# Two-layer encoder block: the mixer's products from rows without the norm, and a convolution shared between VectorE and ScalarE

## What is computed

```python
def rms_norm(x, g):
    xf = x.astype(jnp.float32)
    y = xf * lax.rsqrt(jnp.mean(xf * xf, axis=-1, keepdims=True) + RMS_EPS)
    return (y * g.astype(jnp.float32)).astype(x.dtype)
...
  h = RMSNorm(x)
  one combined input projection of h -> columns partitioned into
    [diff-attn q | diff-attn k | diff-attn v | ssd z | ssd xBC | ssd dt (2 directions) | gate_attn | gate_ssd]
...
        q = rms_norm(q.reshape(b, s, ATTN_HEADS, 2, ATTN_HEAD_DIM), qk_norm_g[i, 0])
        k = rms_norm(k.reshape(b, s, ATTN_HEADS, 2, ATTN_HEAD_DIM), qk_norm_g[i, 1])
...
    u = lax.conv_general_dilated(xbc, conv_w.astype(xbc.dtype)[:, None, :], (1,), [(pad, pad)],
                                 dimension_numbers=("NWC", "WIO", "NWC"),
                                 feature_group_count=SSM_CONV_CH)
    u = jax.nn.silu(u + conv_b)
```

## Time and profile before

| | |
|---|---|
| median of 3 runs | 1735.32 us (1735.26 to 1735.81) |
| the profiled execution, its own time | 1734.33 us |
| its span, first to last instruction | 1732.5 us |
| PE busy | 1686.1 us, 97% of the span |
| DVE, ACT, POOL busy | 718.0, 683.6, 667.9 us (41, 39, 39%) |
| mixers (about) | 0 to 440 us and 867 to 1300 us |
| DMA mean rate | 305 GB/s; about 427 GB/s in the expert stages |

### The profile page before, as it was taken

The page is one execution under the profiler, slowest core; times in us unless marked ns, Lnnn a source line. Parts: engine busy times, 40 slices in busy tenths (PEclk is TensorE's granted clock), DMA queues, the critical chain, the costliest instruction groups (busy, mean ns, idle before and its releaser), DMA issues.

```text
span 1732.5 us, 23236 instructions
## 1 busy us (share of the span) xinstructions
PE 1686.1 (97%) x8975; PEld 1046.0 (60%) x8975; DVE 718.0 (41%) x1351; ACT 683.6 (39%) x1549; POOL 667.9 (39%) x536
## 2 busy tenths in 40 slices
PE   8999999999999999999899999999999999999997
PEld 6889877787434444343378898777874344444342
DVE  6728788524222222221176287875242222122121
ACT  5565787754211111111156557877541111111111
POOL 7788776895000000000077987768940000000000
PEclk9999999999999999999999999999999999999999
DMA  7454312766999999999954452227589999999997
GB/s 285 184 195 152 141 50 102 284 265 275 408 428 428 427 428 427 426 428 428 424 212 162 179 195 98 84 106 283 233 320 414 427 428 427 427 428 428 426 427 311
DMA packets 44659, 528.47 MB, mean 305 GB/s; under 512 B 4824, under 2 KB 7640, under 8 KB 12288
## 3 DMA queue, kind: packets, MB, share of 16 engines
q1 hardware_dynamic: 44512, 526.89, 74.1%
q0 software_dynamic: 32, 0.02, 0.0%
HBM read 525.82 MB, written 1.06 MB: 304 GB/s over the span
## 4 chain that ended last, share of the span: by engine, by line
PE 70%; DMA 13%; DVE 9%; ACT 5%; issue 2%; POOL 1%; SPq 0%; DVEq 0%; ACTq 0%
PE PS L1286 19%; DMA view<-in_w_exp_up_dram 12%; PE PS L1317 11%; PE PS L870 8%; PE PS L872 8%; PE PS L871 8%; DVE view L1987 5%; PE PS L1232 3%; PE PS L1218 2%; DVE view L1983 1%; PE PS L1077 1%; PE PS L1219 1%; ACT view L1555 1%; DMA wr<-in_w_router_dram 1%; PE PS L858 1%
## 5 line engine op out<-in xcount | busy, mean ns | idle before, releaser
L2368 POOL TENSOR_TENSOR view<-view,view 128x512 fp32r<-128x512 f32 x448 | 579.8, 1317 | 543.2 <-ACT view L1441 532.4
L1286 PE MATMUL PS<-view,view 128*64 128x512 f32 x2044 | 455.4, 595 | 19.2 <-DMA view<-in_w_exp_gate_dram 9.9
L1441 ACT ACTIVATE view<-view 128x512 fp32r<-128x512 f32 x448 | 274.5, 631 | 150.7 <-PE PS L872 147.7
L1286 PEld LDWEIGHTS PS<-view,view 128*64 128x64 f32 x2044 | 143.1, 137 | 301.3 <-issue 263.5
L870 PE MATMUL PS<-view,view 128*128 128x512 f32 x704 | 285.4, 405 | 5.1 <-POOL view L2368 3.2
L872 PE MATMUL PS<-view,view 128*128 128x512 f32 x704 | 275.1, 391 | 0.0
L871 PE MATMUL PS<-view,view 128*128 128x512 f32 x704 | 274.9, 391 | 0.0
L2268 DVE SCALAR_TENSOR_TENSOR view<-PS,gcol,view 128x512 fp32r<-128x512 f32 x64 | 48.0, 751 | 476.3 <-ACT view L1754 459.0
L1317 PE MATMUL PS<-view,stb 128*64 128x512 f32 x1024 | 227.7, 596 | 4.4 <-ACT stb L1730 1.5
L1317 PEld LDWEIGHTS PS<-view,stb 128*64 128x64 f32 x1024 | 70.3, 137 | 137.3 <-issue 125.6
L870 PEld LDWEIGHTS PS<-view,view 128*128 128x128 f32 x704 | 132.5, 188 | 32.6 <-issue 5.1
(11 more groups left out here) (263 smaller groups left out, 2028.1 us busy)
## 6 DMA issues: line engine op xcount, KB each, us to landing
view<-in_w_exp_up_dram SPq DMA_DIRECT2D x60, 2048.0 KB, 26.9
view<-in_w_exp_gate_dram SPq DMA_DIRECT2D x60, 2048.0 KB, 26.9
view<-in_w_mix_dram SPq DMA_DIRECT2D x54, 2048.0 KB, 7.6
view<-in_w_exp_down_dram SPq DMA_DIRECT2D x54, 2048.0 KB, 28.8
view<-in_w_exp_down_dram SPq DMA_DIRECT2D x16, 1024.0 KB, 23.9
view<-in_w_mix_dram SPq DMA_DIRECT2D x8, 512.0 KB, 17.9
view<-in_w_exp_gate_dram SPq DMA_DIRECT2D x2, 1792.0 KB, 9.4
view<-bias_table SPq DMA_DIRECT2D x2, 1536.0 KB, 11.8
```

The costliest lines, as they stand in the source:

```text
L1286: ins = pe.matmul(bank(ph, name, j)[e * CAP:(e + 1) * CAP, :], xgT1[:, k, at + e * CAP:at + (e + 1) * CAP], weight_rows(j, kind, row, 1), ...
L1441: nc.scalar.activation(highs(chunk), weights(slot8, chunk), ACT.Copy).then_inc(*high_ready.up(ph))
L2368: g_.tensor_tensor(weights(low8, chunk), weights(slot8, chunk), highs(chunk), ALU.subtract).then_inc(*low_ready.up(ph))
```

## The change

The transposes take the rows of X as they are, so that r is not needed before the products. r is worked out later, from squares that ACT makes within block 0, and is kept as one column per row tile (`r_tok`). It enters as the scale of ACT's evictions (v, z, gates), in DVE's first step of dt, and not at all for q and k, where the floor of the head norm is multiplied by the mean square instead (`e_tok`). For the convolution, where rows lie along the free axis, PE spreads r over 128 partitions with two matrix instructions in block 1 ("spread"), ACT copies it to `r_cols`, DVE multiplies each tile by it in place in PSUM, ACT makes the centre tap, and DVE makes the outer taps of tile c - 1 after the scaling of tile c. `bridge(7)` becomes `bridge(1)`. POOL no longer waits for the scaled rows.

```diff
@@ PE
-                    pe.wait_ge(*xn_ready.at(ph, 4 if k >= KD // 2 else 2))
-                    transpose2(ph, lambda t: XN[:, t, k * P:(k + 1) * P], ("hT", k))
+                    for t in range(TT):
+                        if l:
+                            pe.wait_ge(*out_of(Phase(l - 1), "s", ALL_PAIRS - 1, t, k // (KD // 2)))
+                        else:
+                            pe.wait_ge(s_x[t], 16)
+                    transpose2(ph, lambda t: X[:, t, k * P:(k + 1) * P], ("hT", k))
...
+                    if b == 1:
+                        pe.wait_ge(*row_ready.at(ph, 1))
+                        pe.wait_ge(*free(ph, "spread"))
+                        for t in range(TT):
+                            ins = pe.matmul(bank(ph, "spread")[:, t * P:(t + 1) * P], r_tok[t].to_broadcast([P, P]),
+                                            ident[:, :], start=True, stop=True)
+                        ins.then_inc(*fill(ph, "spread"))
                     if 1 <= b <= 4 and b != 2:
                         qk_transpose(b - 1)
...
-                    bridge(7)
+                    bridge(1)
@@ ACT
-                if l:
-                    cast(ph, 0, 2)
-                for i in range(2 * TT):
...
-                cast(ph, 2 if l else 0, HIGHS - (2 if l else 0))
+                cast(ph, 0, HIGHS)
...
                     cast(ph, nxt, 2)
+                    for i in range(0 if b else 2 * TT):
...
+                        nc.scalar.activation(sq[:, i * COLS:(i + 1) * COLS], X[:, t, n * COLS:(n + 1) * COLS],
+                                             ACT.Square, accum_out=small[:, i:i + 1]).then_inc(*sumsq.up(ph))
...
-                            if b:
-                                act.wait_ge(*rs_in.at(ph, 1 + b))
+                            act.wait_ge(*rs_in.at(ph, 1 + b))
...
-                                                 ACT.Silu).then_inc(*drain(ph, "p", b, t))
+                                                 ACT.Silu, scale=r_tok[t]).then_inc(*drain(ph, "p", b, t))
...
+                    if b == 1:
+                        act.wait_ge(*full(ph, "spread"))
+                        nc.scalar.activation(r_cols, bank(ph, "spread")[:, 0:TT * P], ACT.Copy).then_inc(*drain(ph, "spread"))
...
+                    if c < CT:
+                        act.wait_ge(*x_scaled.at(ph, c + 1))
+                        nc.scalar.activation(acc[:, c % 3, :], bank(ph, "x", c)[:, 0:TT * P], ACT.Identity,
+                                             scale=vcol[:, CW + 2 * CT + c:CW + 2 * CT + c + 1],
+                                             bias=vcol[:, CB + c:CB + c + 1]).then_inc(*centre_tap.up(ph))
                     e = c - 1
                     if 0 <= e < CT:
                         act.wait_ge(*out_of(ph, "x", e))
@@ DVE
-                    for n in range(2):
-                        for t in range(TT):
-                            v.tensor_scalar(XN[:, t, n * COLS:(n + 1) * COLS], X[:, t, n * COLS:(n + 1) * COLS], r[:, t:t + 1],
-                                            None, ALU.mult).then_inc(*xn_ready.up(ph))
-
+                    each(lambda t: v.tensor_scalar(e_tok[t], st[:, t:t + 1], EPS, None, ALU.mult))
+                    v.tensor_copy(st[:, 80:80 + TT], r).then_inc(*row_ready.up(ph))
+                    dve.wait_ge(*row_ready.made(ph))
...
-                norm_rows()
                 for k in range(KD):
                     low_of(hTh[:, k, :], hTl[:, k, :], ("hT", k), k + 1, vcol[:, G1 + k:G1 + k + 1])
+                norm_rows()
                 if l == 0:
                     head_scales(ph)
...
-                    r = rsqrt(16, 2 + b, HD)
+                    r = rsqrt(16, 2 + b, HD, floor=e_tok)
...
+                def scaled_x(c):
+
+                    x_ = bank(ph, "x", c)[:, 0:TT * P]
+                    dve.wait_ge(*full(ph, "x", c))
+                    v.tensor_tensor(x_, x_, r_cols, ALU.mult).then_inc(*x_scaled.up(ph))
...
+                for c in range(CT + 1):
+                    if c < CT:
+                        scaled_x(c)
+                    if c:
+                        outer_taps(c - 1)
@@ POOL
-                if l:
-                    low(0, 2)
-                pool.wait_ge(*xn_ready.at(ph, 4))
-                low(2 if l else 0, 2 * CHUNKS)
+                low(0, 2 * CHUNKS)
```

More of the change, by code:

```diff
@@ L139, in mixer_fills @@
         f += [(("p", b, t), (2 * b + t) % 4) for t in range(TT)]
+        if b == 1:
+            f += [(("spread",), 4)]
         if 1 <= b <= 4:
@@ L442, in encoder @@
         small = sb("small", [P, 48])
+        r_tok, e_tok = ([st[:, o + t:o + t + 1] for t in range(TT)] for o in (80, 86))
         dtv, av, nac, eac, dend = (dtm[:, i] for i in range(5))
@@ L1822, in link, with rsqrt @@
                     dve.wait_ge(*dve_step.made(ph))
-                def rsqrt(n, count, width, done=None):
+                def rsqrt(n, count, width, done=None, floor=None):
                     var, half, y, a, r = (st[:, o:o + n] for o in (0, 16, 32, 48, 64))
-                    v.tensor_scalar(var, var, 1.0 / width, EPS, ALU.mult, ALU.add).then_inc(*rs_in.up(ph))
+                    if floor is None:
+                        v.tensor_scalar(var, var, 1.0 / width, EPS, ALU.mult, ALU.add).then_inc(*rs_in.up(ph))
+                    else:
+                        v.tensor_scalar(var[:, 0:8], var[:, 0:8], 1.0 / width, floor[0], ALU.mult, ALU.add
+                                        ).then_inc(*dve_step.up(ph))
+                        v.tensor_scalar(var[:, 8:16], var[:, 8:16], 1.0 / width, floor[1], ALU.mult, ALU.add
+                                        ).then_inc(*rs_in.up(ph))
+                        dve.wait_ge(*dve_step.made(ph))
                     dve.wait_ge(*rs_in.made(ph))
@@ L1920, in layer @@
                 dve.wait_ge(*full(ph, "dt"))
-                v.tensor_tensor(X0, PS[:, 4, 0:P].rearrange("p (t h) -> p t h", t=TT),
-                                bc_dt.unsqueeze(1).to_broadcast([P, TT, 64]), ALU.add
-                                ).then_inc(*drain(ph, "dt"))
+                for t in range(TT):
+                    ins = v.scalar_tensor_tensor(out=X0[:, t, :], in0=PS[:, 4, t * 64:(t + 1) * 64], scalar=r_tok[t],
+                                                 in1=bc_dt, op0=ALU.mult, op1=ALU.add)
+                    if t == 0:
+                        ins.then_inc(*dve_step.up(ph))
+                ins.then_inc(*drain(ph, "dt"))
+                dve.wait_ge(*dve_step.made(ph))
                 dve.wait_ge(*out_of(ph, "dt"))
@@ L1970, in layer, with outer_taps @@
                 v.tensor_tensor(ebias, nac, tmp[7], ALU.add).then_inc(*bias_ready.up(ph))
-                for c in range(CT):
+                dve.wait_ge(*out_of(ph, "spread"))
+                def scaled_x(c):
+                    x_ = bank(ph, "x", c)[:, 0:TT * P]
+                    dve.wait_ge(*full(ph, "x", c))
+                    v.tensor_tensor(x_, x_, r_cols, ALU.mult).then_inc(*x_scaled.up(ph))
+                def outer_taps(c):
                     x_ = bank(ph, "x", c)[:, 0:TT * P]
                     a = acc[:, c % 3, :]
-                    def w(j):
-                        return vcol[:, CW + j * CT + c:CW + j * CT + c + 1]
-                    dve.wait_ge(*full(ph, "x", c))
-                    if c >= 3:
-                        dve.wait_ge(*u_ready.at(ph, c - 2))
-                    link(v.tensor_scalar(a, x_, w(2), vcol[:, CB + c:CB + c + 1], ALU.mult, ALU.add))
+                    dve.wait_ge(*x_scaled.at(ph, c + 1))
+                    dve.wait_ge(*centre_tap.at(ph, c + 1))
                     for j in (0, 1, 3, 4):
```

33 lines of the change are left out of this document (18 added, 15 removed).

## The result

The changed kernel takes **1805.26 us** (median of 5 runs, 1801.66 to 1806.58), the kernel before 1735.81 us on the same chip: a ratio of 1.0398, with a 95% interval of 1.0383 to 1.0413. It is 69.5 us slower; 63.9 had been forecast. The profiled execution took 1806.6 us, 72.3 us more than that of before. From here on the rows are those of single profiled executions, which differ by some microseconds in the expert stages even where two programs are the same there; so each step is read from one point of a trace to another that is near.

What follows compares the result with a forecast made beforehand. PE was taken to bound the convolution, at 3.08 us per tile, with a wait for the row factor at the layers' border. Layer terms of +34.6 and +29.3 made +63.9 on 1734.3, so 1799 us by median; range 1786 to 1813.

Steps and rivals of the forecast that it cites:

- The convolution: Convolution tiles: casts queue behind SiLU, taps and scaling, so two tiles take 8.3 us, not 6.2; +23 us per layer.
- Block 1: Transposes of q wait for the row chain and slow small DVE steps; +8.6 us in layer 0, +8.4 in layer 1.
- The first small stall: In block 1, PE gets the first of POOL's six products 1.0 us late, counted within that block's loss.
- The slower clock: After PE's idle gap in block 1, half speed for 3 us of work; +1.5 us per layer, between 0 and 3.5.
- Its end: End of the convolution: the last tile's taps, and so the last SiLU, come later; +1.9 us per layer.
- The front: Layer starts: transposes need only the adds of their half of the columns; -0.4 us in layer 0, -5.5 in layer 1.
- What would show it: Trace signs listed beforehand; at the layers' border, block 0 starting 3.0 us after the first last add, not 8.5.
- Rival 4: Convolution: PE's regular idling halves the clock, 4 us more per two tiles, 1887 us in all; chance 5%.

Runs made afterwards that it cites:

- e2: Changed kernel with ScalarE making SiLU of tile c-2, not c-1, behind the centre tap of tile c; ratio 1.0204.
- e7: Changed kernel with the convolution's centre tap given back to VectorE, outer-tap order kept; 1847.8 us, ratio 1.0651.
- e9: Changed kernel with the centre tap on VectorE and all five taps made of the tile just scaled, not the one before; 1756.6 us, ratio 1.0128.
- e4: Changed kernel with bridge(7) in place of bridge(1) at the end of layer 0; ratio 1.0395.
- e3: Changed kernel with the row factor made early, squares ahead of casts and VectorE's chain ahead of the low parts; ratio 1.0339.
- e5: Changed kernel without TensorE's branch over the overflow code, and without its body, at each layer's end; ratio 1.0355.
- e6: Changed kernel with TensorE's branch kept but the overflow code it jumps over cut to one wait; ratio 1.0363.
- e10: Changed kernel with the edits of e3, e4 and e9 together; ratio 1.0045.
- e8: Changed kernel with the edits of e3, e4 and e7 together; 1831.7 us, ratio 1.0545.
- e11: e10 with the change's short bridge and TensorE's jumped-over overflow code cut to one wait, against the kernel before; ratio 1.0049.

## Why the prediction was right, point by point

- **The convolution** (+23 per layer): 22.9 and 22.8. The pair of tiles was put at 8.3 us and takes 8.25, by the chain that was written down, and e2, e7 and e9 show that it is this chain: the order of the same instructions decides between 73 and 118 us (e9 and e7). The scaling takes 0.43 us (0.34 to the start of the taps behind it) where 0.45 was taken. The place of the stall was wrong: not 2.1 us at every second tile, but 1.13 and 0.47 by turns; from the start of one instruction to the next these are 1.51 and 0.86 us against 0.14 unstalled, which is the same 2.1 per pair. The chain links tile c with c + 2 and so fixes only the sum; in layer 0 the split drifts from 1.14 and 0.47 (at 150.90 and 154.70 us) to 1.03 and 0.56 at the end. Why it is split at all, no run tells; in e7 the whole stall does fall on every second tile.
- **Block 1** (+8.6 and +8.4): +7.4 and +9.0, in the second of which some 1.3 us are the slower clock in block 0 that e4 took away; that this clock would fall at the border too had no term. The small steps at 1.22 us beside POOL are there: in layer 1 ten of them, as forecast, though five in each chain and not six and four. The first small stall, put at 1.0 us, is 0.7. e3 shows that the place of the row chain makes the wait.
- **The slower clock** (+1.5 per layer): +2.3 and +2.1 behind block 1, and in layer 1 the 1.3 us above, within the bounds of 0 to 3.5.
- **Its end** (+1.9): +1.8.
- **The front** is the term that failed. -0.4 in layer 0 was -0.8, within its bounds, but the -5.5 us of layer 1 were -0.1. The step at fault is "the transposes need only the adds of their half of the columns": they also need TensorE's sequencer to be there. In the profile before its jump was hidden, because 6.17 us of bridging stood in the same place and the transposes waited for VectorE by 0.16 us only. I had taken the bridge for cover of the wait for data alone. (The prediction also let all 14 bridging instructions go; two stay, and 5.2 us go.) With a short jump the expected start comes true: block 0 3.0 us after the first of the last adds in e5 (898.99 to 902.00), which is the figure under "What would show it".
- That accounts for 5.4 of the 6.7 us between the 63.9 forecast and the 70.6 seen up to the last products; the rest is spread over the terms above, and over +0.6 and +0.8 us behind the convolution's end, where the forecast had nothing and no run shows a cause. That terms of either sign partly cancel (layer 0's block 1 is 1.2 us under its forecast, layer 1's 0.6 over) is luck. The upper end of the range, 1813, is 2 us less than its own parts give (1799 + 6 + 6 + 4).
- **Rival 4**, the falling clock, was right as a mechanism and wrong in its place: at the change's stalls it doesn't happen, at e7's it does, and costs 1.5 us in each pair of tiles there, some 17 us a layer.

## What to carry to other kernels

Before an operation is moved, write down each engine's turn in order and look for an instruction that waits on the newest result of the bottleneck while the bottleneck's next input is queued behind it; here that order was worth 34 us (e2) to 91 us (e7 against e9), and VectorE's added work itself less than 1 us a layer in the convolution (e9). When a wait is taken off the start of a stage, ask what else ends just below it: filler work and a jump over rarely used code don't show while a data wait covers them. And the stalls that are left over should be kept short: here those of 2.4 us cost the clock as well, those of up to 1.13 us didn't.

## What was not expected of the hardware

- A taken jump over a long body cost TensorE 5.0 us, over a body of one wait nothing that the trace shows (e5 and e6 agree within 0.02 us).
- A small VectorE instruction can wait for several POOL instructions in a row, not for one. In e10 the step at L1859, elsewhere in that chain 0.16 us, took 5.34 us and ended together with POOL's fourth product of a run:

```profile
9.69 5.34 DVE L1859 SCALAR_TENSOR_TENSOR stat<-stat 128x2 f32<-128x2 f32 x1
10.07 4.94 POOL L2405 TENSOR_TENSOR view<-view,view 128x512 fp32r<-128x512 f32 x4
```

  TensorE's first product of block 0 waited 4.46 us for it. The same happened in the profiles of e8 (another step, 4.95 us) and e11 (5.25 us). In e3, with the same order there, it didn't: a copy that began 0.05 us after POOL's run took 1.25 us, where e8's, which began 0.03 us after it, took 4.95. The Trainium skill, page SBUF — State Buffer, section Who interferes with whom, lets the loser block for the whole of the other's instruction; here it was four of them. Why, no run of mine tells.
- The clock fell with the length of the gaps, not with their number: stalls of 0.47 and 1.13 us at every tile left it at 1.00 over 97 us, stalls of 2.4 us at every second tile brought it to 0.84 over the convolution (e7).
